# Merge stage of a hybrid decoder layer: where the conv chunks, unit 1's weights, pair 4's shares and the second half's chunks are issued

## What is computed

```python
    y_ssm = ssd_branch(z, xbc, dt_raw, ssm_conv_w, ssm_conv_b, dt_bias, a_log, d_skip, ssm_norm)
    y_attn = attention_branch(q, k, v) * jax.nn.silu(g_attn)
    y_sc = b_sc * causal_depthwise_conv(c_sc * u, sc_conv_w) * jax.nn.silu(g_sc)
    gates = jax.nn.sigmoid(merge.astype(jnp.float32)).reshape(bsz, s, N_BRANCH, D_MODEL)
    merged = (gates[:, :, 0] * (y_ssm @ p_ssm.astype(y_ssm.dtype)).astype(jnp.float32)
              + gates[:, :, 1] * (y_attn @ p_attn.astype(y_attn.dtype)).astype(jnp.float32)
              + gates[:, :, 2] * (y_sc @ p_sc.astype(y_sc.dtype)).astype(jnp.float32))
```

## Time and profile before

| | us |
|---|---|
| median of 3 runs | 2938.43 |
| lowest and highest run | 2933.14, 2949.33 |
| the profiled execution's own time | 2936.59 |
| its span (first to last instruction) | 2935.0 |
| PE busy | 2812.6 (96%) |
| DVE, ACT, POOL busy | 1592.8, 1238.8, 1587.0 |
| merge stage, first to last PE product | 2336.87 to about 2740.7 |
| output stage, first PE product | 2747.84 |

### The profile page before, as it was taken

How to read it: one execution, slowest core, us unless ns; L and a number is a source line. 1 busy time by engine, 2 the same in 40 slices (tenths; PEclk the granted TensorE clock), 3 DMA queues, 4 the chain that set the end, 5 groups by cost and what they waited for, 6 DMA issues and landing times. The chain is left out here.

```text
span 2935.0 us, 40526 instructions
## 1 busy us (share of the span) xinstructions
PE 2812.6 (96%) x14222; PEld 2374.6 (81%) x14222; DVE 1592.8 (54%) x2525; ACT 1238.8 (42%) x2242; POOL 1587.0 (54%) x1078
## 2 busy tenths in 40 slices
PE   6999999999999999999999999998999988899898
PEld 5788888888877888888877888887999966688787
DVE  6335235896534447865335555555667685653433
ACT  5232234333234443332325555555666653432332
POOL 7678778777767788777754454543111253332000
PEclk8999999999999999999999999999999999999999
DMA  4657336432235455322346464646555377855443
GB/s 122 152 152 240 114 115 170 126 112 87 72 94 172 131 155 133 106 89 72 94 136 181 135 186 143 182 144 214 160 164 156 119 240 234 276 182 172 157 150 107
DMA packets 462803, 436.06 MB, mean 149 GB/s; under 512 B 60737, under 2 KB 403009, under 8 KB 454977
## 3 DMA queue, kind: packets, MB, share of 16 engines
q1 hardware_dynamic: 457904, 416.87, 47.9%
q10 hardware_dynamic: 2448, 8.91, 0.8%
q0 software_dynamic: 2304, 8.39, 0.7%
HBM read 290.99 MB, written 143.13 MB: 148 GB/s over the span
## 5 line engine op out<-in xcount | busy, mean ns | idle before, releaser
L531 PE MATMUL p_acc<-h_kept,w_hi 128*128 128x512 f32 x1216 | 477.4, 393 | 4.8 <-DVE p_stage L737 3.1
L533 PE MATMUL p_acc<-h_kept,w_lo 128*128 128x512 f32 x1216 | 475.5, 391 | 0.0
L532 PE MATMUL p_acc<-h_kept,w_hi 128*128 128x512 f32 x1216 | 474.2, 390 | 0.0
L417 POOL TENSOR_TENSOR w_lo<-p_sums,w_hi 128x512 fp32r<-128x512 f32 x300 | 391.5, 1321 | 134.8 <-ACT w_hi L618 134.8
L618 ACT ACTIVATE w_hi<-p_sums 128x512 fp32r<-128x512 f32 x300 | 189.2, 632 | 477.0 <-PE p_acc L533 451.2
L531 PEld LDWEIGHTS p_acc<-h_kept,w_hi 128*128 128x128 f32 x1216 | 228.8, 188 | 54.3 <-ACT work L577 3.3
L533 PEld LDWEIGHTS p_acc<-h_kept,w_lo 128*128 128x128 f32 x1216 | 228.8, 188 | 49.8
L532 PEld LDWEIGHTS p_acc<-h_kept,w_hi 128*128 128x128 f32 x1216 | 228.9, 188 | 48.7
L531 PE MATMUL p_acc<-p_ops,w_hi 128*128 128x512 f32 x608 | 241.2, 397 | 7.1 <-DVE p_ops L719 7.1
L533 PE MATMUL p_acc<-p_ops,w_lo 128*128 128x512 f32 x608 | 239.0, 393 | 0.0
L532 PE MATMUL p_acc<-p_ops,w_hi 128*128 128x512 f32 x608 | 237.3, 390 | 0.0
(11 more groups left out here) (337 smaller groups left out, 6793.1 us busy)
## 6 DMA issues: line engine op xcount, KB each, us to landing
raw<-w_in SPq DMA_DIRECT2D x100, 512.0 KB, 5.2
p_rawb<-w_in SPq DMA_DIRECT2D x76, 512.0 KB, 5.2
s_qs<-p_stage SPq DMA_DIRECT2D x96, 256.0 KB, 4.0
work<-s_gates SPq DMA_DIRECT2D x48, 512.0 KB, 7.7
s_xbc<-p_stage SPq DMA_DIRECT2D x32, 512.0 KB, 2.6
work<-s_xbc SPq DMA_DIRECT2D x16, 1024.0 KB, 7.0
spare<-s_qs SPq DMA_DIRECT2D x16, 1024.0 KB, 5.4
att_all<-s_att SPq DMA_DIRECT2D x24, 528.0 KB, 5.2
```

The costliest lines, as they stand in the source:

```text
L417: tt(w_lo[:, k], weight(u, k), w_hi[:, k], ALU.subtract).then_inc(w_made, 1)
L531: pe.matmul(bank, hi, ops[k][:, 0, c], start=c == 0, stop=False)
L532: pe.matmul(bank, hi, ops[k][:, 1, c], start=False, stop=False)
L533: last = pe.matmul(bank, lo, ops[k][:, 0, c], start=False, stop=c == 3)
```

## The change

- `load_ahead`, new in attention's SP list: before the third pattern's last store, SP waits for values, keys and orderings to be done with `work`, loads the four conv chunks of the first half into `work` (`first_sc`), waits for POOL's split of unit 0's weights (`handed["w"]`) and loads unit 1's ssm and conv weights. The merge's own issue of these weights and ACT's issues of the conv chunks go. In unit 0, SP issues the gates of lanes 0 and 1 only after the low parts of the chunks that lay in their places.
- ACT's order at the merge's start is ssm chunks 4 to 7, unit 1's weights, conv chunks.
- The weighing is cut in two on DVE (`weigh`, `add_windows`) and ACT (`shares_of_windows`, `scale_windows`). For pair 4, the first part is done in unit 7: on DVE ahead of unit 7's gating, on ACT between unit 8's weights and unit 7's gate, with ACT's scaling behind that gate. POOL's list is unchanged.
- In unit 11 SP issues all 16 chunks of the second half, each branch once its lane of unit 11 is done: ssm ahead of the y_attn store, conv and attention behind it and ahead of unit 11's total. All go straight to their buffers (no `y_ahead`), with eight semaphores of two chunks each. ACT issues no DMA any more. DVE makes eight low parts before unit 11's last lane.

```diff
+def load_weights_of(sp, w, raw, m, branches, loaded):
+    for br in branches:
+        _, p, at, n = BRANCHES[br]
+        sp.dma_start(raw[:, at:at + n], w[p][0, :, m * P:(m + 1) * P].rearrange("(c p) n -> p c n", p=P)
+                     ).then_inc(loaded[at > 0], 16)
+def first_sc(work, c):
+    return work[:].rearrange("p k t -> p (k t)")[:, c * HALF:(c + 1) * HALF]
...
+                def load_ahead():
+                    sp.wait_ge(v_turned, NV * PAIRS)
+                    sp.wait_ge(v_ordered, FIRST * PAIRS)
+                    sp.wait_ge(k_made, 2 * PAIRS + FIRST)
+                    for c in range(4):
+                        sp.dma_start(first_sc(work, c), d["y_sc"][c, :, :HALF]).then_inc(handed["sc_loaded"], 16)
+                    sp.wait_ge(handed["w"], 1)
+                    load_weights_of(sp, w, raw, 1, (0, 1), handed["raw_loaded"])
...
                     for g in range(3):
                         if i + 1 < PAIRS:
                             load_q(i + 1, 0, 2 * i + 2, g)
+                        elif g == 2:
+                            load_ahead()
                         store(i, g)
...
+                def load_y(br):
+                    y, _, at, n = BRANCHES[br]
+                    for c in range(n):
+                        sp.dma_start(y_raw[at + c], d[y][c, :, HALF:]).then_inc(y_loaded[(at + c) // 2], 16)
...
-                load_weights(0, 1)
...
                     for lane, br in lanes(u, k) if merging else ():
+                        if u == 0:
+                            sp.wait_ge(y0_made, FIRST_SC + lane + 1)
                         sp.wait_ge(summed, u + 1 if u < LATE else max(9, 2 * u - (7 if lane == 2 else 8)))
                         load_gate(lane, br, m, 0)
...
+                    if u == SECOND - 1:
+                        sp.wait_ge(acc_made[0], SECOND - 2)
+                        load_y(0)
                     if u >= FULL:
                         sp.wait_ge(gated, pair + 2)
                         sp.dma_start(d["y_attn"][:, :, pair * 2 * P:(pair + 1) * 2 * P].rearrange("b p t -> p b t"), g_t
...
                     elif u == SECOND - 1:
-                        sp.wait_ge(turned, pair + 2)
-                        for c in range(AHEAD):
-                            sp.dma_start(y_ahead[c], d["y_ssm"][c, :, HALF:]).then_inc(ahead_loaded, 16)
+                        sp.wait_ge(acc_made[1], SECOND - 2)
+                        load_y(1)
+                        sp.wait_ge(acc_made[2], SECOND - FULL)
+                        sp.wait_ge(y_stored, 16 * 4 + 16)
+                        load_y(2)
...
-                load_y(1, 0)
-                hi_of_y(0, 0, 1)
+                for c in range(FIRST_Y, SSM_N):
+                    copy(y_hi[c], y_raw[c]).then_inc(y_hi_made, 1)
                 for u in range(SECOND):
+                    split(u + 1, (u + 1) % 2, chunks_of(u + 1), [raw_count(u + 1, part) for part in range(2)])
                     if u == 0:
-                        hi_of_y(1, 0)
-                    split(u + 1, (u + 1) % 2, chunks_of(u + 1), [raw_count(u + 1, part) for part in range(2)])
-                    if u < LATE or u >= FULL:
-                        weights_of_windows(u if u < LATE else u - LATE)
+                        act.wait_ge(handed["sc_loaded"], 64)
+                        for c in sc_raw:
+                            copy(y_hi[c], sc_raw[c]).then_inc(y_hi_made, 1)
+                    if u < LATE or u > FULL:
+                        shares_of_windows(u if u < LATE else u - LATE)
+                        scale_windows(u if u < LATE else u - LATE)
+                    elif u == FULL - 1:
+                        shares_of_windows(LATE)
                     gates(u, lanes(u, u % 2))
+                    if u == FULL - 1:
+                        scale_windows(LATE)
 
                 act.wait_ge(acc_made[0], SECOND - 2)
-                load_y(0, 1, range(AHEAD, SSM_N))
-                act.wait_ge(ahead_loaded, 16 * AHEAD)
-                for c in range(AHEAD):
-                    copy(y_hi[c], y_ahead[c]).then_inc(y_hi_made, 1)
+                hi_of_y(range(SSM_N))
                 act.wait_ge(acc_made[1], SECOND - 2)
-                load_y(1, 1)
...
+                hi_of_y(range(SSM_N, 12))
                 act.wait_ge(acc_made[2], SECOND - FULL)
-                act.wait_ge(y_stored, 16 * 4 + 16)
-                load_y(2, 1)
-                hi_of_y(1, 1)
-                hi_of_y(2, 1)
+                hi_of_y(range(12, 16))
...
                     if merging:
-                        weigh(pair)
+                        if u != FULL:
+                            weigh(pair)
+                        add_windows(pair)
                     if not merging:
                         n = use_of(k, u)
+                        if u == FULL - 1:
+                            weigh(LATE)
                         gate_lane(k, n)
...
                     if u == SECOND - 1:
-                        lo_of_y(range(6), 12, y1_made)
+                        lo_of_y(range(SSM_N), 12, y1_made)
```

More of the change, by code:

```diff
@@ L1723, in _ @@
                                         ).then_inc(o_taken, 1)
+FIRST_SC = 8
 BRANCHES = [("y_ssm", "p_ssm", 0, 8), ("y_sc", "p_sc", 8, 4), ("y_attn", "p_attn", 12, 4)]
@@ L1758, in merge_branches_stage @@
         y_raw = [lo.bitcast(F32) for lo in y_lo]
-        y_ahead = [att_all[:, c * HALF:(c + 1) * HALF] for c in range(AHEAD)]
+        sc_raw = {FIRST_SC + c: first_sc(work, c) for c in range(4)}
+        w_ahead = [att_all[:, c * HALF:(c + 1) * HALF] for c in range(W_AHEAD)]
         att_loaded, g_loaded, low_made, ex_made, step, ex_scaled, part_made, part2_made, o_half, o_made, ya_hi_made = (
@@ L1972, in _, with hi_of_y @@
                 copy = lambda to, of: act.activation(to, of, ACT.Copy)
-                def load_y(br, half, chunks=None):
-                    y, _, first, n = BRANCHES[br]
-                    for c in chunks or range(n):
-                        act.dma_start(y_raw[first + c], d[y][c, :, half * HALF:(half + 1) * HALF]
-                                      ).then_inc(y_loaded[(first + c) // 4], 16)
-                def hi_of_y(br, half, part=None):
-                    _, _, first, n = BRANCHES[br]
-                    for c in range(first, first + n) if part is None else range(4 * part, 4 * part + 4):
-                        if br or half:
-                            act.wait_ge(y_loaded[c // 4], 64 * (half + 1) if br == 1 else 64)
+                def hi_of_y(chunks):
+                    for c in chunks:
+                        act.wait_ge(y_loaded[c // 2], 32)
                         copy(y_hi[c], y_raw[c]).then_inc(y_hi_made, 1)
@@ L2004, in split, with shares_of_windows, scale_windows @@
                     copy(w_hi[:, k, at], raw_of(u if at.start == 12 else 0, at)).then_inc(w_hi_made, 1)
-                def weights_of_windows(pair):
+                def shares_of_windows(pair):
                     act.wait_ge(low_made, pair + 1)
                     act.activation(ex[:], low[:], ACT.Exp, scale=-1.0).then_inc(ex_made, 1)
+                def scale_windows(pair):
                     act.wait_ge(ex_scaled, pair + 1)
@@ L2131, in weigh, with add_windows @@
                     tt(ex[:], ex[:], den[:].unsqueeze(2).to_broadcast([P, 2, 3, SLOTS]), ALU.mult).then_inc(ex_scaled, 1)
+                def add_windows(pair):
                     dve.wait_ge(ex_scaled, pair + 1)
@@ L2170, in lo_of_y @@
                         dve.wait_ge(y_hi_made, base + c + 1)
-                        tt(y_lo[c], y_ahead[c] if base and c < AHEAD else y_raw[c], y_hi[c].bitcast(F32), ALU.subtract
+                        tt(y_lo[c], y_raw[c] if base else sc_raw.get(c, y_raw[c]), y_hi[c].bitcast(F32), ALU.subtract
                            ).then_inc(made, 1)
@@ L2196, in _ @@
                         add_attention(k, 2, use_of(2, u))
-                lo_of_y(range(6, 16), 12, y1_made)
+                lo_of_y(range(SSM_N, 16), 12, y1_made)
                 with dve.Fori(0, NM // 2) as i:
@@ L2398, in build @@
             att_all = k.sb("att_all", [P, 2 * TILES * (PAIR + 4)])
-            handed = {n: k.sem("handed_" + n) for n in ("w_hi", "w", "y_hi", "y0")}
+            handed = {n: k.sem("handed_" + n) for n in ("w_hi", "w", "y_hi", "y0", "sc_loaded")}
+            handed["raw_loaded"] = k.sems("handed_raw_loaded", 2)
             att_stored, stored = k.sems("att_stored", 3), k.sems("total_stored", 2)
```

15 lines of the change are left out of this document (6 added, 9 removed).

## The result

| | before | after |
|---|---|---|
| median | 2938.43 (5 runs, 2933.14 to 2949.33) | 2921.05 (5 runs, 2917.10 to 2924.21) |
| ratio, 95% interval | | 0.9937 (0.9914 to 0.9959) |
| the profiled execution's own time | 2936.59 | 2921.05 |
| its span | 2935.0 | 2919.2 |

The account below looks back on a forecast made before the run. TensorE, busy 96% of the 2935.0 us span, bounds the kernel; only its idle time and half-clock products can be won. 5 + 3 + 9.5 = 17.5 us off 2938.4 gives 2921; range 2912 to 2934.

Parts of the forecast that it names:

- Part 1, predicted 5: Merge start: conv chunks and unit 1's weights loaded from attention's end bring unit 0's transposes 5 us earlier; bounds 1.4, 8.9.
- the barrier 3 to 5 us late: Merge start: SP, held by a full queue, reaches the stage's barrier late, so PE starts 3 to 5 us later.
- the weighing in 8.7 us: Unit 0: DVE's weighing of pair 0 takes 8.7 us, since POOL's split of unit 1's weights is over by then.
- the late start hidden: Merge start: PE's later start doesn't count by itself, because unit 0's transposes wait for VectorE's weighing anyway.
- the store's landing: Attention's end: the third pattern's store, queued behind chunks and weights, lands at 2347, four us later than before.
- The rule on completion order: Third store: a DMA's semaphore write follows all earlier writes of its DMA engine, so the store can't overtake chunks and weights.
- Part 2, predicted 3: Before unit 8's transposes: pair 4's shares one unit ahead cut the gap from 7.59 to 4.6, 3 us; bounds 0, 7.6.
- POOL what is late next: Before unit 8: POOL, its order unchanged, ends its split at 2467.9, then needs about 4.5 us for three steps, until 2472.4.
- Part 3, predicted 9.5: Units 12 and 13: SP issuing the second half's chunks by lane brings 9.5 us; bounds 5 and 11.7.
- The rivals that a part brings nothing: Early loads hold back the store, bringing 0 to 1 us (15%); pair 4's early shares bring 0 (10%).
- unit 12's gates: Rival, 15%: these gates, behind attention chunks, or POOL's split hold PE at unit 13; SP's chunk issue brings 4 to 5.
- one queue: Rival, 5%: SP's queue alone moves less than two queues, so the kernel gets 16.5 us slower, 2955.

Follow-up runs that it names:

- e5: Changed kernel with only the four conv chunks loaded early, unit 1's weights again issued at the merge's head; 2920.83 us, ratio 0.9947.
- e4: Changed kernel with the same six early loads issued before the first pattern's last store instead of the third's; 2914.94 us, ratio 0.9931.
- e8: Changed kernel with the early loads before the first pattern's last store and POOL weighing pair 4 before splitting unit 9's weights; 2908.58 us, ratio 0.9885.
- e6: Changed kernel with POOL weighing pair 4 ahead of its split of unit 9's weights; 2917.58 us, ratio 0.9924.
- e2: Changed kernel with pair 4's early weighing undone, so pair 4 is weighed wholly in unit 8; 2925.80 us, ratio 0.9969.
- e7: Changed kernel with the second half's four conv chunks issued by ACT on its own queue instead of by SP; 2924.58 us, ratio 0.9954.
- e1: Changed kernel with the early loads undone: conv chunks and unit 1's weights issued at the merge's start again; 2926.10 us, ratio 0.9972.
- e3: Changed kernel with the second half's chunk issue undone: ACT issues 13 of 16 chunks, SP the first three last; 2929.61 us, ratio 0.9980.
- the second trace of the changed kernel: The changed kernel measured and traced once more, nothing edited, against the kernel before in a new group; 2922.90 us, ratio 0.9955.

## Why the prediction was right

It said 2921, the runs gave 2921.05. Closeness to this degree is luck: the terms were 5 + 3 + 9.5, and the landmarks of the merge give 2.7 to 3.3 + 6.0 + 8.9.

**Part 1, predicted 5 (5.5 before rounding), was 2.7 at T0 in the traces and 3.2 in the medians.** That SP stands about 4 us, the barrier 3 to 5 us late (4.9), the weighing in 8.7 us (2359.02 to 2367.64: 8.6) with a first step near 0.2 (0.17), the conv gap gone and the late start hidden: all as worked out. The step that was mis-sized is the store's landing. It was put at 2347; less the 2.4 us by which A came later it landed at 2349.6. The estimate took the bytes at 384 and 302 GB/s; in the first part of SP's stand on the p_sc load the rate was far lower. A window of the changed kernel, in which SP is at that load for all but the first 0.7 us:

```profile
2337.40:2340.10 2.70, 0.00 (x0) 0.00 (x0) 0.12 (x1) 0.00 (x0) 0.00 (x0) 1.00 0.85 130
```

The 16 DMA engines are 85% busy and move 130 GB/s. The short rows of the weights (128 float32 each) are not the reason: the packets of this window are 98, 3.6 KB each on average, and e5 has such a stretch before any of these weights was issued:

```profile
2332.00:2334.60 2.60, 0.00 (x0) 0.00 (x0) 0.37 (x1) 0.00 (x0) 0.00 (x0) 0.99 0.95 118
```

In e4 the same chunks, with no stores just ahead of them, moved at 307 to 442 GB/s (2291 to 2295). What slows them behind the second pattern's stores stays open. The other 0.2 us are att's way to DVE, 7.0 instead of 6.8. The rule on completion order that the prediction cited from the Trainium skill ("DMA: Bandwidth & Descriptors", Queues, rings and completion order) fits: the store took 10.3 us behind the loads, and 6.3 in e4 and 7.8 before with none in front. No run tests it alone, since shared bandwidth delays the store too: in e5 it took 13.0 us with only the chunks in front and the weights behind. The weighing's gain came through as said: DVE's first step on 128x16 takes 0.17 us with POOL idle and took 2.36 beside POOL's split; timeline of DVE after, then of POOL:

```profile
2350.33 7.23 DVE L2203 TENSOR_TENSOR b_ylo<-work,b_yhi 128x1024 fp32r<-128x1024 f32 x4 [0.63 <-ACT b_yhi L2009]
2359.02 0.17 DVE L2142 TENSOR_TENSOR b_top<-att_all 128x16 f32<-128x16 f32 x1 [1.46 <-DMA att_all<-s_att]
```

```profile
2348.90 3.07 POOL L1971 TENSOR_TENSOR key_lo<-b_raw,key_hi 128x1024 fp32r<-128x1024 f32 x1 [11.88 <-ACT key_hi L2009]
```

The contention moved onto the four conv subtractions, 7.23 us for four where the four ssm ones take 4.63; of the four, the slowest takes 2.73 us and the quickest, after POOL's split, 1.21. Here that is hidden behind the wait for att. In e4 and e8, where att lands earlier, it isn't: DVE goes from the subtractions (7.22 us) to the weighing without idle time. The Trainium skill ("SBUF — State Buffer", Who interferes with whom) names this pair: a VectorE instruction with two SBUF inputs and a GpSimd instruction that reads SBUF contend. The trace agrees, at 2.6 us over four subtractions.

**Part 2, predicted 3, was 6.0 in this trace and 2.9 in the medians.** The mechanism stands as told: exponentials at 2453.78 (2455 was said), DVE's half done at 2462.3 (2465), and POOL what is late next, as the releaser of the gap shows. Mis-sized were two terms. POOL was done 47.2 us after T3, where 2472.4 means 48.2 after it: its split ended as said, its three steps took 3.6 us, not 4.5, with DVE's own adds over by then (in e6, beside them, two of the steps take 1.68 and 1.63 us instead of 1.28 and 1.27). So T8 came 4.0 us earlier after T3 (47.3 instead of 51.3). And the clock, which the sum left out here: windows of 4 us behind the transposes of unit 8, the kernel before and then the changed one:

```profile
2475.46:2479.46 4.00, 4.00 (x14) 3.52 (x15) 3.05 (x3) 1.59 (x2) 0.00 (x0) 0.50 0.01 2
```

```profile
2470.57:2474.57 4.00, 4.00 (x22) 3.46 (x23) 2.73 (x3) 0.00 (x0) 0.00 (x0) 1.00 0.76 204
```

Before, the products behind the gap ran at the 1.2 GHz level, after at 2.4 GHz, and from T8 to T9 it took 22.7 us instead of 24.7: two more. The medians' 2.9 is less, but this trace was a favourable one: over the seven traces with the early shares and POOL's old order, T9 - T3 is 69.3 to 72.9, on average 71.2, against 76.0 before and 75.4 in e2, which makes 4.5. The medians' interval reaches to 6.0 and to nothing, so they don't decide.

**Part 3, predicted 9.5, was 8.9 from T11 to O (9.4 to S12), 6.7 in the medians.** Gap before unit 12 at 2.92 (two to three were said), no gap over 1 us before unit 13 (0.26), chunk pairs 2.5 us apart (2.7 were said) at 413 GB/s (384). The rivals on unit 12's gates and on one queue fell with the 0.26 us gap and with e7. SP did stand once more, 5.46 us on the conv chunks, unforeseen, but the attention chunks behind it weren't issued for another 5.6 us anyway.

**The sum.** The rivals that a part brings nothing fell by e1, e2 and e3, each of which is slower than the changed kernel at its own landmark. The changed kernel was 17.4 us ahead in its first measurement and 13.25 in its second; the two intervals overlap (0.9914 to 0.9959, and 0.9941 to 0.9969). They lie on both sides of the 0.5% that the prediction named as the limit of what can be told.

## What to carry to other kernels

Price a moved DMA by what it will be queued behind and what is queued behind it: an issue of 0.4 to 0.6 us became 3.6 to 6.9 us of a standing SyncE when two to four megabytes of chunks lay in front, and moving the same six loads from before the third store to before the first brought 6.5 us on top of the 2.7 that the move itself had brought. After speeding up an engine's part, look at the engine whose order was not changed: here that was POOL, and one exchanged pair of steps closed the rest of the gap. And where unedited stages scatter by as much as the gain, compare traces from a landmark next to the edit, not from the start.

## What was not expected of the hardware

The length of a gap alone doesn't tell whether the clock falls. Over the nine traces that have an idle stretch before T8, the granted clock of the first 4 us behind it was: before 0.50 (gap 7.59), e2 0.50 (4.58), e1 0.50 (3.70), but e7 1.00 (3.45) and the second trace of the changed kernel 1.00 (3.27), and then e3 0.61 (2.32), e4 0.60 (2.32), e5 0.60 (2.34), against 1.00 (2.30) in the first trace of the changed kernel. A value between 0.50 and 1.00 is a stretch with both levels in it. Window of e4, with a gap 0.02 us longer than the changed kernel's above:

```profile
2456.34:2460.34 4.00, 4.00 (x15) 3.37 (x16) 2.56 (x3) 0.00 (x0) 0.00 (x0) 0.60 0.71 188
```

Where the clock fell, T8 to T9 took 24.2 to 25.3 us, and 22.7 where it didn't: a stall of 2.3 us costs either 2.3 or about 4. What decides it is not settled by these runs. The earlier gap near 2440 behaves alike: in the 4 us behind it the clock was 1.00 in four traces (gaps of 1.83 to 2.41) and 0.57 to 0.68 in the other eight (1.95 to 3.15), and the products up to the idle time before T8 then took 1.5 us longer. Where PE has to wait for POOL before T8 anyway, that time is hidden in the wait: the gap is 2.3 us in the traces with the slow stretch and 3.3 to 3.7 in those without. It means that a single trace can be off by 1.5 to 2.6 us for each such gap, and that a gap closed altogether, as in e6 and e8, can be worth more than its length.
